# Attention scores from queries held as high over low halves, in a fused two-layer kernel on Trainium2

## The reference

```python
kc = rms_norm(compress(k_c, cmp_pos_k, w_cmp_k), k_norm_g[0])      # 15 compressed keys per group
vc = compress(v_c, cmp_pos_v, w_cmp_v)
s_c = einsum('bsgrd,bcgd->bgrsc', q, kc) * SCALE - slopes * dist_c  # compressed branch
p_c = masked_softmax(s_c, dist_c >= 0)
o_cmp = einsum('bgrsc,bcgd->bsgrd', p_c, vc)
# selected branch: with 256 rows all blocks are selected, so a causal softmax over k_s, v_s
# window branch:   the window of 512 covers all 256 rows, the same over k_w, v_w
o_nsa = g[:, :, 0] * o_cmp + g[:, :, 1] * o_slc + g[:, :, 2] * o_win
```

## Time and profile before

| | |
|---|---|
| Median of 3 runs | 902.04 us (901.62 to 902.25) |
| Profiled execution | 901.26 us, its span 899.2 us |
| TensorE busy | 892.7 us, 99% of the span, 4926 matmuls |
| VectorE busy | 706.0 us, 79% |
| ScalarE busy | 555.3 us, 62% |
| Granted TensorE clock | full speed in all 40 slices |

### The profile page before, as it was taken

One profiled execution on the slowest core, in us unless ns is written; L12 is line 12 of the kernel. 1 busy time (PEld: TensorE's weight loads), 2 busy tenths in 40 slices (PEclk: granted clock), 3 DMA queues, 4 the chain that ended last, 5 costly groups with the idle time before them and its releaser, 6 DMA issues.

```text
span 899.2 us, 13582 instructions
## 1 busy us (share of the span) xinstructions
PE 892.7 (99%) x4926; PEld 767.0 (85%) x4926; DVE 706.0 (79%) x1381; ACT 555.3 (62%) x954; POOL 43.2 (5%) x54
## 2 busy tenths in 40 slices
PE   9999999999999999999999999999999999999997
PEld 7988877888888888888889998888889988888886
DVE  6888899789866666677998999999976786666665
ACT  7767878755644444456655657776745755754454
POOL 0410000000000000000010100100000000000000
PEclk9999999999999999999999999999999999999999
DMA  9977677676465555556798888487565377555551
GB/s 343 320 214 199 177 203 219 198 293 202 154 229 187 192 191 196 190 191 209 219 236 268 231 206 270 106 230 240 169 211 164 114 212 237 187 187 187 188 188 47
DMA packets 97218, 184.53 MB, mean 205 GB/s; under 512 B 8128, under 2 KB 18176, under 8 KB 96896
## 3 DMA queue, kind: packets, MB, share of 16 engines
q1 hardware_dynamic: 92128, 166.35, 56.1%
q0 software_dynamic: 4656, 16.78, 10.0%
q10 hardware_dynamic: 368, 0.52, 0.2%
HBM read 164.69 MB, written 1.05 MB: 184 GB/s over the span
## 4 chain that ended last, share of the span: by engine, by line
PE 99%; ACT 1%; issue 0%; DVE 0%; DVEq 0%; ACTq 0%
PE pb L523 97%; PE pb L527 1%; PE pb L738 1%; ACT SM L1400 0%; ACT wlo L1174 0%; ACT SM L1174 0%; ACT whi L1174 0%; ACT PTC L1174 0%; DVE XS L2617 0%; DVE XS L2625 0%; DVEq L59 0%; DVE DG L2359 0%; ACT MSQ L1757 0%; DVE ST L2603 0%; ACT CC L1174 0%
## 5 line engine op out<-in xcount | busy, mean ns | idle before, releaser
L1174 ACT ACTIVATE whi<-raw 128x1024 fp32r<-128x1024 f32 (+2 forms) x304 | 309.1, 1039 | 125.5 <-PE pb L523 112.5
L1787 DVE TENSOR_TENSOR wlo<-raw,whi 128x1024 fp32r<-128x1024 f32 (+1 forms) x267 | 315.7, 1211 | 78.7 <-ACT whi L1174 78.2
L523 PE MATMUL pb<-XT,whi 128*128 128x512 f32 (+1 forms) x1232 | 283.8, 358 | 0.0
L523 PE MATMUL pb<-whi,ZO 128*128 128x512 f32 (+1 forms) x776 | 238.9, 388 | 0.0
L523 PEld LDWEIGHTS pb<-XT,whi 128*128 128x128 f32 x1232 | 200.8, 189 | 23.8 <-issue 1.4
L523 PEld LDWEIGHTS pb<-whi,ZO 128*128 128x128 f32 x776 | 145.2, 188 | 29.7 <-issue 0.4
L523 PE MATMUL pb<-XT,wlo 128*128 128x256 f32 (+1 forms) x1032 | 166.4, 282 | 0.0
L523 PEld LDWEIGHTS pb<-XT,wlo 128*128 128x128 f32 (+1 forms) x1032 | 153.2, 190 | 14.0
L523 PE MATMUL pb<-whi,XT 128*128 128x512 f32 (+1 forms) x544 | 161.8, 389 | 0.0
L523 PE MATMUL pb<-wlo,ZO 128*128 128x512 f32 (+1 forms) x388 | 148.3, 387 | 0.0
L523 PEld LDWEIGHTS pb<-whi,XT 128*128 128x128 f32 x544 | 101.0, 188 | 20.7 <-issue 0.7
(11 more groups left out here) (258 smaller groups left out, 657.9 us busy)
## 6 DMA issues: line engine op xcount, KB each, us to landing
raw<-in_w_in SPq DMA_DIRECT2D x105, 512.0 KB, 4.8
raw<-in_w_ff SPq DMA_DIRECT2D x64, 512.0 KB, 5.3
raw<-in_w_up SPq DMA_DIRECT2D x32, 512.0 KB, 4.5
raw<-in_w_down SPq DMA_DIRECT2D x32, 512.0 KB, 4.8
wlo<-raw POOLq DMA_DIRECT2D x31, 512.0 KB, 5.8
raw<-in_w_branch_b SPq DMA_DIRECT2D x8, 512.0 KB, 5.3
raw<-in_w_out SPq DMA_DIRECT2D x8, 512.0 KB, 4.1
raw<-in_wx_kv SPq DMA_DIRECT2D x8, 512.0 KB, 5.4
```

The lines of the kernel that those rows point to most:

```text
L523: return e.matmul(o, l, r, start=start, stop=stop, skip_group_check=True)
L1174: return e.activation(o, i, ACT.Copy, scale=scale)
L1787: e.tensor_tensor(wlo[u % NW][:, 0:c], raw_tile(u)[:, 0:c], whi[u % NW][:, 0:c].bitcast(F32), ALU.subtract).then_inc(lo, 1)
```

## The change

- Each query head is kept in float32r as high part and low part, one on 64 partitions and the other on the other 64, in `OT` (`q_cols`); for each group the keys' high parts and low parts lie on both halves (`k_cols`). A matmul over all 128 rows then gives (high + low) times the key's high part, a second adds the low part's.
- For the first query tile the matmul takes the 128 keys of both kinds at once and is made with the first pair (b = 0) only. VectorE reads the part it needs from the bank (`a` in `negated`).
- High parts are made by ScalarE (now 4 copies of 64 partitions for each n = 1, 2, 3), low parts by VectorE (`qk_low` in steps 5, 6, 9, 4 instructions each). TensorE turns at steps 1, 3, 4, 7. POOL doubles the keys by two DMAs of 64 partitions with 1024 columns each.
- The compressed scores move from step 7 to 12, in 16 float32r matmuls of 32 columns; their softmax moves from steps 8, 9, 10 to 13, 14, 16, their turning from 12 to 18. The bias is loaded straight into `PC`, to which VectorE adds the scores in 8 instructions instead of 2.
- Values go in twos: pairs 0 and 1 at step 22, 2 and 3 at 29, 4 and 5 at 35, 6 and 7 at 42.
- The third pair (n = 2) is turned by VectorE in steps 21 and 22; there is a third buffer `PT`.

```diff
+        def q_cols(f, p):
+            return slice(512 * f + 256 * p, 512 * f + 256 * p + 256)
+        def k_cols(g, l, b):
+            a = 2048 + 1024 * g + 512 * l + 256 * b
+            return slice(a, a + 256)
...
-        values_of = {a: (i,) for i, a in enumerate(pair_at[3:] + (35,))}
-        values_of[42] = (6, 7)
-        blocks_of = {pair_at[n] + 5 + i: (n, i) for n in (3, 4, 5, 6, 7) for i in range(3)}
-        by_pe = [j for j in range(16) if j // 2 not in (3, 4, 5, 6, 7)]
+        values_of = {22: (0, 1), 29: (2, 3), 35: (4, 5), 42: (6, 7)}
+        blocks_of = {pair_at[n] + 5 + i: (n, a, b) for n in (3, 4, 5, 6, 7)
+                     for i, (a, b) in enumerate(((0, 6), (6, 11), (11, 16)))}
+        blocks_of[pair_at[2] + 5], blocks_of[pair_at[2] + 6] = (2, 0, 8), (2, 8, 16)
+        by_pe = [j for j in range(16) if j // 2 not in (2, 3, 4, 5, 6, 7)]
...
@@ SP
-                    e.dma_start(CB[:, :], A["consts2"]).then_inc(cb_in, 16)
+                    e.dma_start(PC[:, :], A["consts2"][:, 0:512]).then_inc(cb_in, 16)
+                    e.dma_start(CB[:, 512:1024], A["consts2"][:, 512:1024]).then_inc(cb_in, 16)
...
@@ TensorE
-                    for n in ((), (0, 1), (2,), (3,))[s] if s < 4 else ():
+                    for n in {1: (0,), 3: (3,), 4: (1,), 7: (2,)}.get(s, ()):
...
-                    if s == 7:
+                    if s == 12:
...
-                                i = mm(PB[7][:, a:a + 64], TT[:, TQ + f, t * P:t * P + P], KCT[:, :],
-                                       t == 0 and f == 0, t == 1 and f == 3)
+                                for p in range(2):
+                                    a, g = 256 * t + 64 * f + 32 * p, f // 2
+                                    i = mm(PB[7][:, a:a + 32].rearrange("p (l n) -> p l n", l=2),
+                                           OT[:, q_cols(f, p)][:, t * P:t * P + P], kcs[:, :, 15 * g:15 * g + 16],
+                                           a == 0, a == 480)
-                    if s == 12:
+                    if s == 18:
...
-                            mm(PB[4 + p][:, 0:128], TT[r, TQ + f, 0:128], TT[r, k[p], 0:128], True, False)
-                            mm(PB[4 + p][:, 128:384], TT[r, TQ + f, 128:256], TT[r, k[p], 0:256], False,
-                               True).then_inc(sc_done, 1)
+                            o, q = PB[4 + p], OT[:, q_cols(f, p)]
+                            for l in range(2) if b == 0 else ():
+                                kinds = OT[:, 2048 + 1024 * g + 512 * l:2560 + 1024 * g + 512 * l].rearrange(
+                                    "p (b n) -> p b n", b=2)
+                                mm(o[:, 0:256].rearrange("p (b n) -> p b n", b=2), q[:, 0:128], kinds[:, :, 0:128],
+                                   l == 0, False)
+                            mm(o[:, 256:512], q[:, 128:256], OT[:, k_cols(g, 0, b)], b == 1, False)
+                            mm(o[:, 256:512], q[:, 128:256], OT[:, k_cols(g, 1, b)], False, True).then_inc(sc_done, 1)
...
@@ ScalarE
+                        for j in range(2):
+                            for p in range(2):
+                                r = slice(64 * p, 64 * p + 64)
+                                o = OT[r, q_cols(2 * n - 2 + j, p) if n < 3 else k_cols(p, 0, j)]
+                                i = copy(o, PB[(4, 4, 6, 5)[n]][r, 256 * j:256 * j + 256], qk_gain(n, j, r))
+                        i.then_inc(qk_hi, 1)
-                    if s == 9:
+                    if s == 14:
+                    if s == 13:
+                        scale_p(0, 0)
...
@@ VectorE
+            def qk_low(n):
+                e.wait_ge(qk_hi, (1, 2, 3, 1)[n])
+                for j in range(2):
+                    for p in range(2):
+                        r, q = slice(64 * p, 64 * p + 64), slice(64 - 64 * p, 128 - 64 * p)
+                        c = q_cols(2 * n - 2 + j, p) if n < 3 else k_cols(p, 0, j)
+                        o = OT[q, c] if n < 3 else OT[r, k_cols(p, 1, j)]
+                        i = e.scalar_tensor_tensor(out=o, in0=PB[(4, 4, 6, 5)[n]][r, 256 * j:256 * j + 256],
+                                                   scalar=qk_gain(n, j, r), in1=OT[r, c].bitcast(F32),
+                                                   op0=ALU.mult, op1=ALU.subtract)
+                i.then_inc(qk_lo, 1)
...
-                    if s == 8:
+                    if s == 13:
...
+                        for l in range(2):
+                            if l:
+                                after_step()
+                            for g in range(2):
+                                for q in range(2):
+                                    d = pc[:, :, q, 2 * g:2 * g + 2, 15 * g:15 * g + 15]
+                                    step(e.tensor_tensor(d, cs[:, :, 2 * g:2 * g + 2, q, l, 0:15], d, ALU.add))
-                    if s == 10:
+                    if s == 16:
...
-                            e.wait_ge(pv_done, 2 * n - 2)
-                        for m in range((0, 6, 11)[part], (6, 11, 16)[part]):
+                            if n > 2:
+                                e.wait_ge(pv_done, 2 * n - 4)
+                        for m in range(first_block, end_block):
...
@@ POOL
-            for n, i, done in ((1, TC, kc_swapped), (4, TK, ks_swapped)):
-                e.wait_ge(qk_out, n)
+            e.wait_ge(kc_copied, 1)
...
+            e.wait_ge(qk_lo, 1)
+            for g in range(2):
+                r, q = slice(64 * g, 64 * g + 64), slice(64 - 64 * g, 128 - 64 * g)
+                k = OT[:, 2048 + 1024 * g:3072 + 1024 * g].bitcast(F32)
+                e.dma_start(k[q, :], k[r, :]).then_inc(ks_doubled, 16)
```

More of the change, by code:

```diff
@@ L106, in build, with pt1 @@
         SMP = [work(W0 + 10480 + 768 * i, f"SM{i}", 768) for i in range(2)]
-        PTP = [work(W0 + a, f"PT{i}", 768) for i, a in enumerate((12016, 14840))]
+        PTP = [work(W0 + a, f"PT{i}", 768) for i, a in enumerate((12016, 14840, 7216))]
         SM, PT = ([v[i // 2][:, 384 * (i % 2):384 * (i % 2) + 384] for i in range(4)] for v in (SMP, PTP))
-        SM2, PT2 = ([v[i][:, :].rearrange("p (c n) -> p c n", c=6) for i in range(2)] for v in (SMP, PTP))
+        SM2, PT3 = ([v[:, :].rearrange("p (c n) -> p c n", c=6) for v in b] for b in (SMP, PTP))
+        def pt1(j):
+            return PTP[j // 2 % 3][:, 384 * (j % 2):384 * (j % 2) + 384]
         CC = [work(W0 + a, f"CC{i}", 1024)[:, :].rearrange("p (f n) -> p f n", f=4) for i, a in enumerate((12784, 16240))]
@@ L407, in build, with qk_gain, key_tile @@
             "cross_scores", "cross_max", "cross_exp", "cross_p", "cross_p_turned", "cross_p_copied", "cross_summed"))
-        TQ, TK, TC = 0, 4, 8
-        def key_tile(first_tile, w, g, half):
-            return first_tile + w + 2 * (g != half)
+        def qk_gain(n, j, r):
+            a = PRM["kg"] + 1 + j
+            return PR[r, a:a + 1] if n == 3 else QG[r, 2 * n - 2 + j:2 * n - 1 + j]
+        def key_tile(w, g, half):
+            return w + 2 * (g != half)
         pair_at = (10, 13, 16, 19, 22, 26, 29, 32)
@@ L879, in attention1 @@
                         n = pair_of[s]
-                        f, k = n // 2, [key_tile(TK, n % 2, n // 4, p) for p in range(2)]
-                        e.wait_ge(qk_out, 4)
-                        e.wait_ge(ks_swapped, 32)
+                        f, b, g = n // 2, n % 2, n // 4
+                        e.wait_ge(qk_lo, 2 if f < 2 else 3)
+                        e.wait_ge(ks_doubled, 32)
                         if n:
@@ L1381, in attention1 @@
                             exps(2 * pair_of[s - 2] + p, 0)
-                    if s - 4 in pair_of:
+                    if s == 13:
+                        scale_p(0, 0)
+                    if s - 4 in pair_of and s > 14:
                         scale_p(2 * pair_of[s - 4], 0)
@@ L2006, in attention1 @@
                                 r = slice(64 * half, 64 * half + 64)
-                                v = TT[r, key_tile(TC, w, g, half), 16 * half:16 * half + 240].rearrange(
+                                v = TT[r, key_tile(w, g, half), 16 * half:16 * half + 240].rearrange(
                                     "p (c j) -> p c j", j=16)
@@ L2024, in attention1 @@
                         for b in range(4):
-                            i = e.transpose(KCT[32 * b:32 * b + 32, 32 * (b // 2):32 * (b // 2) + 32],
-                                            KCN[0:32, 32 * b:32 * b + 32])
+                            i = e.transpose(KCT[32 * b:32 * b + 32, :], KCN[0:32, 32 * b:32 * b + 32])
                         step(i)
                         after_step()
-                        e.tensor_scalar(KCT[:, :], KCT[:, :], prm("kg"), None, ALU.mult).then_inc(kct_out, 1)
+                        step(e.tensor_scalar(KCS[:, 0:32], KCT[:, :], prm("kg"), None, ALU.mult))
+                        after_step()
+                        e.scalar_tensor_tensor(out=KCS[:, 32:64], in0=KCT[:, :], scalar=prm("kg"),
```

(2 more changed lines are left out.)

88 lines of the change are left out of this document (41 added, 47 removed).

## The result

The changed kernel takes 911.98 us (median of 4 runs, 911.33 to 913.01) against 902.14 for the kernel before beside it: 9.8 us slower, ratio 1.0111 (95% interval 1.0096 to 1.0127). The forecast was 907.5 and the range ended at 910.6. The direction was right, the size too small. The profiled execution took 911.71, its span 909.8, which is 10.6 more than before.

The account below looks back on a forecast made before the run. TensorE was taken as the bound, with nearly full VectorE stalling it at bank hand-overs. VectorE +7.2 us (-1.8 + 11.4 - 2.4), less 0.4 slack, about 6.8 at ga0, less 1.35 saved later: +5.5, median 907.5; 8-in-10 range 902.9 to 910.6.

Parts of the forecast that it names:

- up to the outputs of c1 it costs nothing, and these outputs come 1.8 us earlier: VectorE ahead of c1: low parts fit idle time and the moved softmax's place, so c1's outputs come 1.8 us earlier.
- turning queries and keys in four groups instead of three: TensorE's account, early attention steps: the extra group of turns costs nothing.
- its own 1.6 to 1.9 each: VectorE, steps 5, 6 and 9: four low-part instructions in a row take 1.6 to 1.9 us.
- the stretch c1 to b1: VectorE between outputs of c1 and b1: 11.4 us more work, 2.4 absorbed by idle time; 9.0 longer.
- over 95% busy: Sign to look for: VectorE busy for over 95% from step 12 to 23.
- TensorE's account: TensorE in the attention: 3.3 us saved if nothing waits, 1.35 of it after step 23.
- Merging: TensorE, value products of two pairs together: three merges save 0.15 us each, 0.45 in all.
- no new wait behind ga0: Pair seven, behind ga0: VectorE's maxima still come in time, with 0.5 us left.
- The DMAs of the doubled keys: POOL's two doubling copies after step 5, needed at step 10: cost nothing, at most 1 us ahead of c1.
- Rival 3: Lag goes on: ScalarE waits for VectorE's step 13, more waits at x1 to b0 and pair seven; 910.0, chance 0.10.
- rival 4: Scores: float32r matmul with two-part moving operand runs at half rate, 0.24 for 0.119; 910.4, chance 0.06.
- its 311 ns: Third pair's transposes: page figure for 128x128 would make six tiles 1.9 us and the sum +1.4; the row says 6.0.

Follow-up runs that it names:

- the clearing moved too: Changed kernel, 9 of 12 low-part instructions left out and VectorE's memset of two UU1 columns put behind x0's outputs: 909.62 us, +7.7.
- the clearing moved alone: Changed kernel, whole, with VectorE's memset of two UU1 columns put behind x0's outputs: 910.57 us, +8.6.
- steps 28 and 36: Kernel before with 16 idle block transposes on VectorE, eight each in these steps, where ScalarE frees the banks: 903.26 us, +1.5.
- sixteen idle transposes: Kernel before with 16 block transposes on VectorE whose result nobody reads, eight each in steps 21 and 22: 908.02 us, +6.3.
- the idle low parts: Kernel before with 12 unused low-part instructions on VectorE in steps 5, 6, 9: 905.89 us; with third pair turned by VectorE too: 912.52 us.

## Why the prediction was wrong in size

Executions differ by up to 1.2 us before the attention begins, so the points below are counted from TensorE's start of step 0: 34.30 before, 34.47 after; 34.89 with the low parts left out, 34.15 with the clearing moved too, 34.83 with the clearing moved alone; and with the third pair on TensorE 34.53, then 34.89 (low parts left out, clearing moved) and 34.52 (clearing moved). Up to c1 the kernels with the third pair on TensorE are the same programs as those without, so each cell but one has two executions. Each entry gives TensorE's waits ahead of c1, the start of c1's outputs against the kernel before, and the whole time against it:

| | clearing ahead of x0's outputs | clearing behind them |
|---|---|---|
| low parts made | waits 2.7, outputs +1.4, time +9.8 | waits 0.3, outputs -1.0, time +8.6 |
| the same, third pair on TensorE | 1.3, +0.1, +3.0 | 0.2, -1.1, +2.0 |
| low parts left out | 1.4, +0.2, +10.7 | 0, -1.6, +7.7 |
| the same, third pair on TensorE | (not run) | 0.8, -0.7, +2.1 |

- **Failed: "up to the outputs of c1 it costs nothing, and these outputs come 1.8 us earlier".** They came 1.4 later, 3.2 from the forecast. Without TensorE's waits of 2.7 ahead of c1 they would have come 1.3 earlier, so most of the 1.8 was there (-1.6 where no wait stood), and the waits took it. Three things make them, and their shares are known only in part.
  - The clearing's wait for the fourth turned group. Moving the clearing gave 1.2, 1.0 and, with the low parts left out, 3.0 us. I had costed "turning queries and keys in four groups instead of three" at nothing, by TensorE's time, and had not asked who counts these turns.
  - The low parts. They take 1.97 a group, and the two groups in steps 5 and 6 had to fit into the 3.0 us of idle time that the forecast named; its own 1.6 to 1.9 each would not have fitted either. With the clearing behind, x0's outputs begin 26.3 and 26.1 after step 0 with them, 24.7 and 25.6 without. But TensorE has no wait over 0.2 for that at x0 to c1, and leaving them out then gave 0.9 in one pair of runs (each interval over 1 us to either side) and nothing in the other. So what they cost here is not told from nothing. And ahead of the clearing's wait removing them gave nothing, since VectorE stood still there anyway.
  - The wait at c0 to x0. TensorE now turns two groups ahead of x0 instead of four and gets there 12.2 us after step 0 instead of 12.8, so it can meet VectorE's additions. The wait was 0.84 in the kernel after. With the low parts left out and the clearing moved it was 0 in one execution and 0.83 in the other of what is the same program up to there, so 0.9 us at c1 can lie between two executions. This wait stands in none of the forecast's terms.
- The profiled execution of the changed kernel is a late one. VectorE waited 1.99 us for the swap of the compressed keys, 0.44 in the run with the third pair on TensorE, whose program is the same up to there. GpSimd issued the swap 8.9 us after step 0 against 7.9, and it took up to 7.3 us to land against 6.3. The c1 outputs are 1.3 later than in that run. This is in the 10.6 of the span, and need not be in the 9.8 of the medians.
- **Right: the stretch c1 to b1.** 9.4 for 9.0. It is 52.1 in the four changed kernels with the third pair on VectorE and the low parts in steps 5, 6 and 9, and 47.0 in the three with it on TensorE, against 42.7 before: 5.1 for the pair, 4.3 for the softmax and what goes with it. (With one low group in step 8 it is 50.3, because c1's outputs are later.) VectorE's busy time there went from 35.7 to 46.6, 10.9 more for 11.4 forecast, and its idle time from 7.1 to 5.5, so 1.5 was absorbed, 2.4 forecast: two misses that cancel in part. That it would be over 95% busy was too much: 89%, and 97% in the last window.
- **Missed: the clock.** The forecast's sum knew only the wait of 5 us, not the 1.5 us of half speed behind it.
- **Half right: TensorE's account.** Pairs 0.96 and 0.49, compressed scores 1.7: as forecast. Merging brought nothing measurable for 0.45. In all TensorE saved 2.1 for 3.3 (11.0 of waits, 1.5 by the clock and 0.2 of later start would make 12.7, the spans differ by 10.6), of which after ga0 1.3 for 1.35.
- Right: no new wait behind ga0; TensorE does not wait at pair seven. The DMAs of the doubled keys cost nothing. Rival 3 did not show: in the changed kernel TensorE waits nowhere for ScalarE. Nor did rival 4: the float32r matmuls run at 0.12 each.
- On turning by VectorE the trace agrees with the rule of the Trainium skill, page "VectorE: DVE Perf Modes", section "Rules for kernel authors", to turn 128x128 on TensorE where PSUM will do: the pair's 0.84 us on TensorE against 7.0 in the end here. But steps 28 and 36 show that the price is one of place: 16 such instructions cost 1.5 there. On the figure the prediction went too far: the Trainium skill, same page, section "The three transpose paths", gives its 311 ns for bf16. The tiles here are float32, so the trace does not test it.

The sum again for the profiled execution: forecast 5.5, plus 3.2 at c1, 0.4 in the stretch and 1.5 by the clock, less 0.2 as VectorE's lateness of 10.8 made ga0 only 10.2 later (0.6 of slack for 0.4), plus 0.2 of later start, is 10.6, as the spans say. The median is 0.8 less, 9.8; the late swap of this one execution may be the reason, but no run shows it.

## What to carry to other kernels

When a step moves, look up every semaphore it raises and read who waits for it, also in parts of the program that the diff leaves alone; a wait that was long satisfied can become the bound. A load on a secondary engine costs by its place: ahead of the instruction that frees a bank it counted nearly in full here, in steps 28 and 36 a quarter. If removing a suspect changes nothing, a second one may stand behind it: remove both before acquitting either.

## What the hardware did that I had not expected

TensorE's granted clock fell to half (the lower level, 1.2 GHz) behind some idle stretches of a few microseconds, each time for 3.4 us. The fall does not wait for the work: in the kernel after it comes 0.4 us before TensorE works again, with the clearing moved 1.4 us after. In windows (columns as above), first the kernel after, whose ga0 starts at 127.34, then the one with the clearing moved, whose ga0 starts at 125.33:
```profile
126.50:126.90 0.40, 0.00 (x0) 0.00 (x0) 0.40 (x3) 0.40 (x3) 0.00 (x0) 1.00 0.79 87
126.94:127.30 0.36, 0.00 (x0) 0.00 (x0) 0.33 (x2) 0.36 (x3) 0.00 (x0) 0.57 0.78 171
```
```profile
125.33:126.80 1.47, 1.47 (x5) 0.94 (x6) 1.42 (x4) 1.47 (x5) 0.00 (x0) 0.98 1.11 298
126.90:130.10 3.20, 3.20 (x9) 2.52 (x8) 3.10 (x9) 0.49 (x2) 0.00 (x0) 0.50 0.56 113
```
So the price at ga0 differs: 1.4 to 1.6 us where the low stretch began in the wait, 1.7 with sixteen idle transposes, and 2.0 in the second kernel shown (14 matmuls in 4.92 for 2.96).

After waits of up to 1.54 us the clock stayed at 1.00. After 3.60, 3.63, 4.25, 4.99, 5.00, 5.05 (twice) and 5.06 us it fell each time. Between, it goes either way: it stayed after 1.79, 1.84 (three times), 2.46 and 2.63 us, and fell after 1.80, 1.84 and 2.65. The same wait at b0 to b1 was 1.84 with the low parts left out, at full clock behind it (first row), and 1.84 again with the clearing moved too, with a fall behind it (second and third):
```profile
106.92:110.22 3.30, 3.30 (x18) 2.90 (x19) 3.20 (x8) 3.11 (x4) 0.50 (x1) 1.00 0.32 123
```
```profile
102.60:104.43 1.83, 0.00 (x1) 0.03 (x1) 1.73 (x5) 1.60 (x5) 0.00 (x0) 1.00 0.45 79
104.43:107.80 3.37, 3.37 (x11) 2.84 (x12) 3.27 (x8) 3.18 (x4) 0.58 (x1) 0.55 0.30 112
```
A fall need not cost anything. In this last kernel the one at b1 made TensorE's work from b1 to ga0 1.45 us longer (15.96 for 14.51), VectorE came no later for it, and the next wait, at ga0, was 3.60 in place of 5.05.

The wait of the idle low parts at c1 to x1 was 2.65 and the clock behind it 0.57 in one kernel, 2.63 and 1.00 in the other, with the same work ahead:
```profile
79.23:82.60 3.37, 3.37 (x12) 2.84 (x13) 3.19 (x9) 1.67 (x5) 0.00 (x0) 0.57 0.73 230
```
```profile
78.98:82.20 3.22, 3.22 (x20) 2.87 (x21) 3.04 (x9) 1.67 (x5) 0.00 (x0) 1.00 0.69 219
```
The first kernel's five times go with this: 904.4 and 904.5 at a mean clock of 1.000, 905.9, 906.5 and 907.5 at 0.998. What decides in this middle range was not settled. Neither was why the swap DMA took the longer in one execution.
